# Second attention of a diffusion backbone: other banks for the first products and maxima, other places for maxima, squares and casts

## The reference

```python
q_lat = apply_rope(gqa_queries(h_lat, q_g), cos, sin)      # 12 heads of 64, each rms-normed
k_lat = apply_rope(k_lat, cos, sin)                        # 4 key heads, 3 query heads share one
s_ctx = jnp.einsum('bqkgd,bckd->bkgqc', qi, k_ctx) * scale
s_win = jnp.where(valid, jnp.einsum('bqkgd,bskd->bkgqs', qi, ki) * scale, NEG_INF)   # |distance| <= 128
p = jax.nn.softmax(jnp.concatenate([s_ctx, s_win, sink_col], axis=-1), axis=-1)
o = p[..., :n_ctx] @ v_ctx + p[..., n_ctx:n_ctx + span] @ v_win
```

## Time and profile before

| | |
|---|---|
| median of three runs | 3478.05 us (3477.78 to 3481.8) |
| profiled execution | 3480.53 us, span 3478.7 us |
| TensorE busy over the span | 3196.2 us (92%) |
| VectorE, ScalarE, POOL busy | 1579.8 us (45%), 1015.1 us (29%), 467.3 us (13%) |
| mean granted clock of TensorE | 0.956 |
| second attention: first product's matmul to the loop's first scores | 2277.66 to 2323.83 us |
| its loop, to the last values product | 2323.83 to about 2620 us |

### The profile page before, as it was taken

One profiled execution on the slowest core, in us unless ns is written; L12 is line 12 of the kernel. 1 busy time (PEld: TensorE's weight loads), 2 busy tenths in 40 slices (PEclk: granted clock), 3 DMA queues, 4 the chain that ended last, 5 costly groups with the idle time before them and its releaser, 6 DMA issues. The chain is left out here.

```text
span 3478.7 us, 37648 instructions
## 1 busy us (share of the span) xinstructions
PE 3196.2 (92%) x14242; PEld 2182.5 (63%) x14242; DVE 1579.8 (45%) x1955; ACT 1015.1 (29%) x1363; POOL 467.3 (13%) x367
## 2 busy tenths in 40 slices
PE   5697999999987999999999978869998899999998
PEld 0273333333366888888888856734446688888887
DVE  1222554454335454444445563345543555555554
ACT  1113455555522212111121231024443321221221
POOL 0000354545500000000000000024440000000000
PEclk7798899999999999999999989979999999999999
DMA  9610000000030111111111001000001111111111
GB/s 408 262 51 17 4 4 3 2 3 2 0 109 31 43 37 36 36 37 41 36 36 36 31 13 42 31 15 1 1 1 49 50 61 36 48 60 36 48 60 49
DMA packets 34908, 162.23 MB, mean 47 GB/s; under 512 B 3889, under 2 KB 6705, under 8 KB 24754
## 3 DMA queue, kind: packets, MB, share of 16 engines
q1 hardware_dynamic: 34834, 161.24, 12.8%
HBM read 157.03 MB, written 4.19 MB: 46 GB/s over the span
## 5 line engine op out<-in xcount | busy, mean ns | idle before, releaser
L613 PE MATMUL PS<-f_uh,f_Wh 128*128 128x512 f32 (+1 forms) x1760 | 483.2, 372 | 25.7 <-DVE f_ul L351 24.9
L613 PE MATMUL PS<-f_ul,f_Wh 128*128 128x512 f32 (+1 forms) x1760 | 481.5, 371 | 0.0
L613 PE MATMUL PS<-f_uh,f_Wl 128*128 128x512 f32 (+1 forms) x1760 | 481.2, 371 | 0.0
L762 DVE SCALAR_TENSOR_TENSOR X<-PS,mod,X 128x512 f32<-128x512 f32 (+1 forms) x440 | 306.2, 698 | 306.6 <-PE PS L613 306.6
L613 PEld LDWEIGHTS PS<-f_uh,f_Wh 128*128 128x128 f32 x1760 | 308.1, 188 | 89.7 <-issue 19.5
L613 PE MATMUL PS<-f_gh,f_WDh 128*128 128x512 f32 (+1 forms) x880 | 330.3, 375 | 19.5 <-DVE f_gl L748 17.2
L613 PEld LDWEIGHTS PS<-f_ul,f_Wh 128*128 128x128 f32 x1760 | 308.7, 188 | 59.0
L613 PEld LDWEIGHTS PS<-f_uh,f_Wl 128*128 128x128 f32 x1760 | 308.3, 188 | 59.1
L613 PE MATMUL PS<-f_gl,f_WDh 128*128 128x512 f32 (+1 forms) x880 | 325.0, 369 | 0.0
L613 PE MATMUL PS<-f_gh,f_WDl 128*128 128x512 f32 (+1 forms) x880 | 324.9, 369 | 0.0
L731 DVE SCALAR_TENSOR_TENSOR part<-PS,part,part 128x1023 f32<-128x1023 f32 (+1 forms) x132 | 130.0, 1012 | 328.6 <-ACT part L668 328.6
(11 more groups left out here) (255 smaller groups left out, 4318.7 us busy)
## 6 DMA issues: line engine op xcount, KB each, us to landing
mod_w<-in_mod_w SPq DMA_DIRECT2D x48, 1024.0 KB, 13.5
part<-in_w_up SPq DMA_DIRECT2D x88, 512.0 KB, 3.5
part<-in_w_down SPq DMA_DIRECT2D x22, 1024.0 KB, 5.5
part<-in_w_out SPq DMA_DIRECT2D x16, 512.0 KB, 3.5
X<-in_xT SPq DMA_DIRECT2D x4, 1280.0 KB, 9.6
X<-in_xT SPq DMA_DIRECT2D x1, 5120.0 KB, 16.1
part<-in_wqk SPq DMA_DIRECT2D x8, 512.0 KB, 3.5
out<-X SPq DMA_DIRECT2D x16, 256.0 KB, 2.0
```

The costliest lines, as they stand in the source:

```text
L613: mm = pe.matmul(ps(bank + c, hi - lo), w_, x_[:, lo:hi], start=f_, stop=l_)
L762: dve.scalar_tensor_tensor(out=X[:, m, lo:hi], in0=ps(DNB[r % 2], hi - lo), scalar=moda(layer, 5, m, 0 if lo < SEQ else 1), in1=X[:, m, lo ...
```

## The change

What it does: products 1 and 2 of group 0 get banks of their own (`FREE`), and TensorE's wait for the product before them goes (for product 3 it becomes a wait for product 0). The first row of maxima uses banks 2, 3 and 4, 5 in turn. The fifth product of group 0 moves from ahead of the loop to pairs 0 to 2, and the second row of maxima of that group stretches to pair 4. All other maxima move to `STEADY`; the squares of the later products go from side 0 to side 1, and POOL casts before it adds. The wait on `mc` is counted by what TensorE has issued.

```diff
+            FREE = {1: (0, 1), 2: (2, 3)}
...
+            def product(pair, G, w):
+                at(pair - 1, 1 if pair > 1 else 0, "sq", G, w)
+                at(pair, 0, "nt", G, w)
+                at(pair, 1, "ro", G, w)
+                at(pair + 1, 0, "ca", G, w)
+
+            def maxima(G, jj, places, row):
+                for t_, (pair, side) in enumerate(places):
+                    at(pair, side, "max", G, jj, t_)
+                at(row, 0, "mn", G, jj)
+                at(row, 1, "row", G, jj)
+            EARLY = [(0, 0), (0, 1), (1, 0), (1, 1), (2, 0), (2, 1), (3, 0), (4, 0)]
+            STEADY = [(0, 0), (0, 1), (1, 0), (2, 0), (2, 1), (3, 0), (3, 1), (4, 0)]
...
                 o = NP_ * G
                 for w, r in enumerate((-15, -13, -9, -7, -3)):
-                    at(o + r - 1, 0, "sq", G, w)
-                    at(o + r, 0, "nt", G, w)
-                    at(o + r, 1, "ro", G, w)
-                    at(o + r + 1, 0, "ca", G, w)
+                    product(o + r if G else 1 if w == 4 else UPFRONT - 1, G, w)
                 for jj, r in enumerate((-8, -2, 4)):
-                    early = o + r == -2
-                    for t_ in range(8):
-                        if early:
-                            at(t_ // 2, t_ % 2, "max", G, jj, t_)
-                        else:
-                            at(o + r + (0, 1, 2, 2, 3, 3, 4, 4)[t_], (1, 1, 0, 1, 0, 1, 0, 1)[t_], "max", G, jj, t_)
-                    at(4 if early else o + r + 5, 0, "mn", G, jj)
-                    at(4 if early else o + r + 5, 1, "row", G, jj)
+                    if G == 0 and jj < 2:
+                        maxima(G, jj, EARLY if jj else [(UPFRONT, 0)] * 8, 4 if jj else UPFRONT)
+                    else:
+                        maxima(G, jj, [(o + r + d, side) for d, side in STEADY], o + r + 5)
...
+                def banks(G, w):
+                    return FREE.get(NW * G + w, (NB, TB))
+
+                def max_bank(G, jj, qt):
+                    return 2 if (G, jj) == (0, 0) and qt % 2 else RB
...
+                            casts(NU * n + u, 0)
                             add(n, u)
-                            casts(NU * n + u, 0)
...
-                        at_least(pe, "out", q)
+                        at_least(pe, "out", q if q > 3 else max(q - 2, 0))
...
-                        at_least(pe, "mc", 24 * G + 8 * jj + qt)
+                        done["max"] += 1
+                        at_least(pe, "mc", done["max"] - (2 if (G, jj) == (0, 0) else 1))
...
                         pe.wait_ge(s["mn"], R + 1)
+                        at_least(pe, "mc", done["max"])
```

More of the change, by code:

```diff
@@ L1707, in _ @@
                         for u in range(NU):
+                            casts(NU * n + u, 0)
                             add(n, u)
-                            casts(NU * n + u, 0)
                 @block.tensor
                 def _(pe):
-                    done = {"nt": 0, "row": 0, "spread": 0}
+                    done = {"nt": 0, "row": 0, "spread": 0, "max": 0}
                     def qk(n, u):
@@ L1770, in norms @@
                         pe.wait_ge(s["sq"], q + 1)
-                        at_least(pe, "out", q)
+                        at_least(pe, "out", q if q > 3 else max(q - 2, 0))
                         at_least(pe, "fin", done["spread"])
-                        pe.matmul(ps(NB, hi - lo), bones, sq[q % 2][:, :hi - lo], start=True, stop=True)
-                        pe.matmul(ps(TB, hi - lo), rot1[:, 1 - t_, :], QK1[:, 2 * G + t_, lo:hi],
+                        nb, tb = banks(G, w)
+                        pe.matmul(ps(nb, hi - lo), bones, sq[q % 2][:, :hi - lo], start=True, stop=True)
+                        pe.matmul(ps(tb, hi - lo), rot1[:, 1 - t_, :], QK1[:, 2 * G + t_, lo:hi],
                                   start=True, stop=True).then_inc(s["nt"], 1)
@@ L1779, in maximum @@
                         pe.wait_ge(s["cast"], NW * G + (3 if jj == 0 else 4 if qt < 4 else 5))
-                        at_least(pe, "mc", 24 * G + 8 * jj + qt)
+                        done["max"] += 1
+                        at_least(pe, "mc", done["max"] - (2 if (G, jj) == (0, 0) else 1))
                         at_least(pe, "mr", done["row"])
+                        rb = max_bank(G, jj, qt)
                         q = qb[JS[jj]][:, qt * P:(qt + 1) * P]
@@ L1785, in maximum @@
                         nk = (hi - lo) * P
-                        pe.matmul(ps(RB, BANK)[:, CTX:BANK], q, k[:, SEQ:T], start=True, stop=True)
-                        pe.matmul(ps(RB + 1, nk), q, k[:, lo * P:hi * P], start=True, stop=False)
+                        pe.matmul(ps(rb, BANK)[:, CTX:BANK], q, k[:, SEQ:T], start=True, stop=True)
+                        pe.matmul(ps(rb + 1, nk), q, k[:, lo * P:hi * P], start=True, stop=False)
                         if qt > 0:
-                            mm = pe.matmul(ps(RB + 1, P), identb[:, :], maskb[:, 0, :], start=False, stop=(qt == 7))
+                            mm = pe.matmul(ps(rb + 1, P), identb[:, :], maskb[:, 0, :], start=False, stop=(qt == 7))
                         if qt < 7:
-                            mm = pe.matmul(ps(RB + 1, nk)[:, nk - P:nk], identb[:, :], maskb[:, 1, :],
+                            mm = pe.matmul(ps(rb + 1, nk)[:, nk - P:nk], identb[:, :], maskb[:, 1, :],
                                            start=False, stop=True)
@@ L1848, in inverse @@
                         at_least(act, "rinv", q)
-                        act.activation(halved(lnb, m), in_halves(ps(NB, m)), ACT.Ln, bias=eps[:, 0:1],
+                        nb, _ = banks(G, w)
+                        act.activation(halved(lnb, m), in_halves(ps(nb, m)), ACT.Ln, bias=eps[:, 0:1],
                                        scale=1.0 / C_HD).then_inc(s["ln"], 1)
                         act.wait_ge(s["ln"], q + 1)
-                        act.activation(in_halves(ps(NB, m)), halved(lnb, m), ACT.Exp, scale=-0.5)\
+                        act.activation(in_halves(ps(nb, m)), halved(lnb, m), ACT.Exp, scale=-0.5)\
                             .then_inc(s["rinv"], 1)
@@ L1947, in rotated @@
                         dve.wait_ge(s["nt"], q + 1)
-                        T_ = ps(TB, m)
+                        nb, tb = banks(G, w)
+                        T_ = ps(tb, m)
                         dve.tensor_tensor(T_, T_, rope[:, 1, lo:hi], ALU.mult).then_inc(s["ts"], 1)
@@ L1959, in rotated @@
                                 op = dve.tensor_tensor(in_halves(dst[0:64, lo:hi]), halved(t1[rows_], m),
-                                                       in_halves(ps(NB, m, rows_)), ALU.mult)
+                                                       in_halves(ps(nb, m, rows_)), ALU.mult)
                         op.then_inc(s["out"], 1)
@@ L1968, in maximum @@
                         lo, hi = WIN[qt]
-                        dve.reduce_max(mc[:, m:m + 1], PS[:, RB * BANK + CTX:(RB + 1) * BANK + (hi - lo) * P], AX_X)\
+                        rb = max_bank(G, jj, qt)
+                        dve.reduce_max(mc[:, m:m + 1], PS[:, rb * BANK + CTX:(rb + 1) * BANK + (hi - lo) * P], AX_X)\
                             .then_inc(s["mc"], 1)
```

## The result

The changed kernel takes 3445.57 us in the median of four runs (3443.59 to 3447.37) against 3479.93 for the kernel before beside it; the ratio is 0.9901, 95% interval 0.9884 to 0.9918. The forecast was 3447.0.

What follows compares the result with a forecast made beforehand. Nothing overlaps ahead of the loop; in it TensorE is the bound, with holes ahead of maxima. 3480.5 profiled −8.9 −6.6 +2.7 −15.0 −3.2 = 3449.5, or 3447.0 us for the median; range 3441.5 to 3455 (0.70).

Steps and rivals of the forecast that it cites:

- Part 1: First products ahead of the loop: own banks save 2.2 us, moving the fifth product away 6.6; together 8.9 us saved.
- Part 2: First maxima ahead of the loop: alternating two bank sets brings reductions from 1.91 to 0.96 us apart; 6.6 us saved.
- Part 3: First head: the fifth product in pairs 0 to 2 is not hidden and opens a hole; net +2.7 us.
- Part 4: Steady loop: new places of the maxima close most holes ahead of them; 15.0 us saved, bounds 10 to 17.
- on VectorE that is what lets the reduction go first: Steady loop: said of squares and turns at the other side of a pair; nothing changes on ScalarE.
- Part 5: Clock in the loop: two falls behind 2.14 us holes go with the holes; 3.2 us saved.
- The single fall more: First head: by the skill's rule alone, holes close together make the clock fall once more; sum 1.6 us higher.
- rival 1: Ahead of the loop: the clock rises there too, saving 6.3 us more, 3441; chance 0.11.
- Holes did not move: Rival 2, in the loop: holes move instead of closing, VectorE's work being unchanged; +10.7 us, 3458; chance 0.14.
- rival 3: Loop: casts hold POOL, so adds come late and ScalarE's exponentials wait; at 3 us each 3492; chance 0.03.

Runs made afterwards that it cites:

- experiment 1: The kernel before with only banks of their own for products 1 and 2 and the shorter wait; 3477.45 us, ratio 0.9993.
- experiment 8: The changed kernel with ScalarE's squares of the next product issued before the inverse of the present one; 3442.80 us.
- experiment 9: The changed kernel with ScalarE's squares ahead of the inverse, but the single banks 6 and 7 and the old wait; one run of 3449.59 us.
- experiment 7: The changed kernel with the first row of maxima in banks 4 and 5 alone; 3452.40 us.
- experiment 6: The changed kernel with the fifth product of the first group back ahead of the loop; 3450.49 us.
- experiment 4: The changed kernel with squares and turns of the later products back at side 0 of their pair; 3448.68 us.
- experiment 5: The changed kernel with POOL's add ahead of the casts again; 3446.34 us.
- experiment 2: The kernel before with only the new places in the steady loop, squares at side 1 and casts ahead of the add; 3464.36 us, ratio 0.9951.
- experiment 10: The changed kernel with squares ahead, plus first-group products and maxima moved and maxima ahead of products in groups 1 to 3; 3436.98 us.
- experiment 3: The changed kernel with the maxima of the steady loop back in their old places, everything else kept; 3460.14 us.

## Why the prediction was right

Its five parts hold in their mechanisms. Set against the two profiles, the parts without the clock came out at 9.8, 6.7, −2.4 and 15.3 us gained where it had 8.9, 6.6, −2.7 and 15.0, the clock in the loop at 5.1 where it had 3.2, and the rest of the span gave 1.4 us back: 33.1 in sum for 31.0. The misses partly cancel, which is luck.

*Part 1 (8.9 us).* Right in its mechanism: ScalarE's order, not the banks, sets products 1 and 3, and experiments 1, 8 and 9 show both waits. The size was 0.9 us short, since product 1 ran partly at the full clock: it took 2.78 us (2284.07 to 2286.85, ScalarE's release) where I had taken 3.65, "if the clock is the same".

*Part 2 (6.6 us).* Right: 6.70 by experiment 7.

*Part 3 (+2.7 us).* Right: the product and its hole cost 4.07 us in experiment 6, 0.4 of them by the clock of the first scores, where I had 1.9 + 2.0, and the hole is 1.92. In pair 4 the rows wait under 0.2 us instead of 2.5, but the maximum just ahead of them waits 1.03, so 1.3 are given back where I had 1.4. The fall of the clock that stood behind the rows before, 1.4 us, is gone too. I had left that fall as it was, and it is more than the error of any of parts 1 to 4 in sum.

*Part 4 (15.0 us).* Right, place by place: the holes that stayed or came are 0.62 three times and 0.1 nine times, for which I had 0.5 and 0.1. Read from start to start the closed holes were 2.2 us longer in sum than the brackets that I had used. The whole account of the loop by its two profiles: holes −16.8 us (26.0 to 9.2), scores and products at the slow clock −5.1, the product added +1.8, and what is left is +2.1: −18.0. Of these 2.1 some 1.4 are turnarounds of 0.05 to 0.1 us that I had not counted, and the rest isn't resolved; they take back what the longer holes gave. Of its three edits, once the new places stand, only these carry anything (experiments 4 and 5); "on VectorE that is what lets the reduction go first" holds for the turns at the old places alone; the casts' order, costed at nothing, costs and brings TensorE nothing.

*Part 5 (3.2 us).* The two falls are gone from the changed kernel, and experiment 2 has no fall behind the first head. That the holes alone made them isn't shown: experiment 1 has the three holes of 2.14 us and a fall behind only one of them. The single fall more, by the rule of the Trainium skill (TensorE: Matmul & The Clock Gate, HAM oscillation) that the prediction weighed, did not come in the changed kernel, nor in experiments 4 to 10; with the same first head it came in experiment 3.

*The rivals.* The clock did not rise over the maxima of the changed kernel: 0.51, and the first scores took 5.79 us; of rival 1 only 0.9 us on product 1 came. Holes did not move, except the one that experiment 10 shows. One sign of rival 3 did appear: in pair 4 of the first head a run of adds stood behind a product's casts and released ScalarE late, in the timeline of the changed kernel:

```profile
2333.24 0.61 POOL L1697 CAST part<-part 64x512 bf16<-64x512 f32 x1
2333.81 4.27 POOL L1713 TENSOR_TENSOR part<-part,part 128x384 f32<-128x384 f32 x4
...
2338.08 0.60 ACT L1901 ACTIVATE part<-PS 128x512 f32<-128x512 f32 x1 [1.07 <-POOL part L1713]
```

Experiment 5, with the add first, has no such wait there. TensorE shows no hole behind it, so the wait cost nothing. In the whole loop POOL released an exponential three times, in the kernel before four times.

## What to carry to other kernels

Where one engine is the bound, list its holes by size and place and ask for each which long instruction stood ahead of its releaser in that engine's queue; moving the small dependent instruction to a pair in which the releaser has no long one closed thirteen holes and shortened three for no work removed, against nine new ones of 0.1 us. When two waits end within a microsecond of each other, doing away with one shows little of what both are worth: here 3.2 and 0 us alone, 6.6 together. And when a wait is moved off one instruction, look whether the next one on that engine waits for the same thing.

## What the runs showed of the hardware

The fall of the clock is not settled by the holes. Experiment 1's loop has the instructions and holes of the kernel before. Its windows, the first head and then behind each of the three holes of 2.14 us:

```profile
2346.40:2353.20 6.80, 6.04 (x10) 2.85 (x11) 1.07 (x2) 1.80 (x3) 1.23 (x1) 0.50 0.01 2
2395.30:2398.30 3.00, 3.00 (x14) 1.73 (x15) 0.92 (x2) 0.98 (x2) 0.39 (x1) 1.00 0.00 0
2471.30:2474.30 3.00, 3.00 (x14) 1.69 (x13) 0.92 (x2) 0.98 (x2) 0.44 (x1) 1.00 0.01 3
2547.90:2551.10 3.20, 3.20 (x9) 1.49 (x8) 0.63 (x2) 0.98 (x2) 0.07 (x1) 0.50 0.00 0
```

So one fall of the two is missing, and the one in the first head lasts twice as long as before; its loop took 297.31 us for 297.49. Likewise, the changed kernel and the one of experiment 3 have the same holes at the head of the loop (1.92, then 0.55); behind them experiment 3 was granted 0.73 (a mean of both levels, 0.50 from 2326.8 us on), the changed kernel 1.00 (the window above from 2320.0 us). The window of experiment 3:

```profile
2325.00:2329.00 4.00, 3.62 (x18) 1.86 (x16) 2.88 (x3) 0.49 (x1) 3.10 (x4) 0.73 0.00 0
```

While the reductions ahead of the loop follow one another, the clock rose in experiment 10 alone, behind a stretch in which TensorE was busy 3.23 of 3.40 us:

```profile
2292.90:2296.30 3.40, 3.23 (x15) 1.70 (x15) 2.34 (x3) 0.00 (x0) 0.00 (x0) 0.50 0.00 0
2296.30:2302.10 5.80, 2.69 (x24) 1.60 (x23) 5.68 (x9) 1.01 (x1) 0.00 (x0) 1.00 0.01 3
```

A turn of 512 columns, which is 0.75 us in the row of experiment 3, can be stretched by POOL. Beside a cast and the add behind it, in the kernel of experiment 4:

```profile
2356.52 1.92 DVE L1956 SCALAR_TENSOR_TENSOR X<-part,sml,part 128x512 f32<-128x512 f32 x1
2356.55 0.39 POOL L1697 CAST part<-part 64x256 bf16<-64x256 f32 x1 [2.32 <-DVE part L1980]
```

Not every neighbour does it: POOL added beside the turn of experiment 3 as well (the turn ran from 2381.81 us), and that turn kept its 0.75 us. What separates the two cases is not settled by these rows.

```profile
2380.88 2.54 POOL L1713 TENSOR_TENSOR part<-part,part 128x384 f32<-128x384 f32 x2 [4.22 <-ACT part L1901]
```

So half of the 1.47 us of the turn ahead of the 2.14 us hole was stretching. A reduction out of PSUM beside casts keeps its 0.82 us, in the changed kernel:

```profile
2322.65 0.82 DVE L1991 TENSOR_REDUCE part<-PS 128x1 f32<-128x640 f32 x1
2322.68 0.60 POOL L1699 CAST part<-part 64x512 bf16<-64x512 f32 x1 [5.55 <-DVE part L1980]
```

The Trainium skill (GPSIMD Engine Reference, Key points) says that POOL shares its SBUF interfaces with VectorE and contends with VectorE's instructions of two SBUF inputs or in a 2-port performance mode; the turn has two, the reduction has one and in PSUM, and the rows beside casts agree. The negation (L1998) reads only one tensor, with a column beside it, and is stretched too: 0.23 us alone (2305.72) and 0.97 beside an add, in the changed kernel. Whether it runs in such a mode no run here shows.

```profile
2352.91 2.14 POOL L1713 TENSOR_TENSOR part<-part,part 128x384 f32<-128x384 f32 x2 [3.62 <-ACT part L1901]
...
2354.11 0.97 DVE L1998 TENSOR_SCALAR part<-part,part 128x8 bf16<-128x8 f32 x1
```
